# Scattering expert results with an add in the transfer, every slot included

## The chip, the cores and the metric

One core of one Trainium2 chip. The metric is the device time of one execution in microseconds (us). Engines are called by their names; the profile writes PE for TensorE's matrix products (PEld for its weight loads), DVE for VectorE, ACT for ScalarE, POOL for GpSimd and SP for SyncE. "SPq" and "POOLq" are the instructions with which an engine issues transfers.

## The reference

One step of a decoder layer for 512 prompt tokens and 8 sample tokens: a mixer of a recurrent and a convolutional group, attention into 256 memory tokens, and a mixture of experts, each followed by a layer norm. Only the experts matter here:

```python
scores = jax.nn.sigmoid(xf @ w_router)                # 520 tokens, 64 experts
...                                                   # 4 of 8 groups, then the 8 best experts
gates = w_sel / jnp.sum(w_sel, axis=-1, keepdims=True) * ROUTED_SCALE
y = swiglu(xf, w1_s, w3_s, w2_s) + routed_experts(xf, idx, gates, w1_e, w3_e, w2_e)
# routed_experts, for each expert e and the tokens that chose it:
hb = jax.nn.silu(xb @ w1_e[e]) * (xb @ w3_e[e])       # 1024 -> 256
out[token] += (hb @ w2_e[e]) * gate                   # 256 -> 1024
```

All data is float32. Each token has 8 experts, so there are 520 x 8 = 4160 results of 1024 numbers (4 KB), and the output of a token is the sum of its 8.

## The kernel before

The experts are taken one after the other, the fullest first in an order that the kernel works out by sorting. A position of that order is "light" or "heavy" by its number modulo 16 (7 of 16 are light). A light expert has 64 slots for tokens, a heavy one 96, the first of all 112. For each expert e the engines do the following, each engine in a fixed order of steps, with counting semaphores between them:

- VectorE compares each token's place in the expert with the slot numbers (`oh_step`), TensorE multiplies that one-hot matrix with a table (`a_step`), and VectorE turns the product into row numbers (`i_step`: `indices` for heavy experts, `indices_few` for light ones). `picked` holds 8 x token + turn - 8192 for a slot with a token, and 0 for an empty one. `idx_y` is that plus `FAR` = 8192, the row of the result table `y_rows`; `idx_x` is `idx_y` shifted right by 3, the token. An empty slot thus has row 8192, which is beyond both tables, and a transfer with a bounds check leaves it out. For a light expert the results lie in two halves on 128 partitions, and the numbers count half rows.
- GpSimd gathers the tokens' rows with an indirect DMA (`g_step`, L746), in two transfers for a heavy expert (64 and 32 slots).
- TensorE transposes them (L859), multiplies with w1 and w3, later with w2 (L844). ScalarE and VectorE empty the results into `ys`, of which there are two.
- GpSimd scatters `ys` into `y_rows` with an indirect DMA (`s_step`): L759 for heavy experts, again in two transfers, L752 for light ones. Each result has a row of its own, so a plain write does. The last three experts are not scattered; their results are multiplied into the sum at the end.

SyncE loads the weights of expert e+4 as soon as TensorE has used those of expert e (`next_in`, L539 and L540, 1 MB each, after the first products; `next_out`, L544, after the last). There are four buffers, tiles of `arena`. GpSimd's order is: scatter e-1, gather e+3, scatter e, gather e+4; both kinds run on its one queue, q0. A `ys` buffer may be written again when the scatter of two experts earlier has landed (semaphores `m_s`, `m_sm`).

SyncE writes zeros over the rows of `y_rows` early (L555, L557), long before the first scatter. At the end SyncE waits for all scatters (L602 and the line before it), reads `y_rows` back in tiles of 128 tokens, and TensorE adds up the 8 rows of each token with a matrix of ones (`sum_rows`); the last layer norm follows tile by tile.

Of the kernel before, what the change touches and what calls it, by code (L numbers as in the profile page):

```python
# [6 lines left out]
ALU = mybir.AluOpType  # L7
ACT = mybir.ActivationFunctionType
AX = mybir.AxisListType
F32 = mybir.dt.float32  # L10
# [4 lines left out]
P = 128  # L15
D = 1024
# [15 lines left out]
NROW = T * TOPK  # L32
FAR = 8192.0
LCAP = 64
# [5 lines left out]
NB = 16  # L40
# [35 lines left out]
           ("swT", "A"), ("x23", "A"), ("sorted", "V"), ("order", "V"), ("x24", "A"), ("rank", "V"), ("count", "V")]  # L76
GROUPS += [(f"so{t}", "V") for t in range(TT)] + [("slots0", "A"), ("slots1", "A")]
GID = {name: g for g, (name, _) in enumerate(GROUPS)}
SORT_CONSTS = 14 + 2 * NB
FIRST = 4  # L80
LAST_ORDER = [0, 4, 1, 2, 3]
SCATTERED = E - 3
# [68 lines left out]
def decoder_step(nc: bass.Bass, ins, outs):  # L151
# [3 lines left out]
    with ExitStack() as ctx:  # L155
        def sb(name, shape, dt=F32):
            return ctx.enter_context(nc.sbuf_tensor(name, shape, dt))

        def sem(name):
            return ctx.enter_context(nc.semaphore(name))  # L160

        x2_rows = nc.dram_tensor("x2_rows", [T, D], F32)
        q_rows = nc.dram_tensor("q_rows", [NS, D], F32)
        y_rows = nc.dram_tensor("y_rows", [NROW, D], F32)

        arena = sb("arena", [P, 3 * 8192])
        act_mem = sb("act_mem", [P, A_SIZE])
# [11 lines left out]
        h0t = sb("h0t", [P, RC, NS])  # L179
        c8 = sb("c8", [P, 8, RC])  # L180
        eps_t = sb("eps_t", [P, 1])
        small = sb("small", [P, 44])
        order = sb("order", [1, E], I32)
        psum = ctx.enter_context(nc.psum_tensor("psum", [P, 4, D], F32))

# [70 lines left out]
        picked = act_mem[:, A4 + 1820:A4 + 1820 + 2 * NB].rearrange("p (n c) -> p n c", c=2)  # L256
        swT = act_mem[:, A4 + 1296:A4 + 1296 + T]
        gates = act_mem[:, A4 + 1860:A4 + 1860 + 2 * NB].rearrange("p (n c) -> p n c", c=2)
        idx_y = sb("idx_y", [P, NB], U32)
        idx_x = sb("idx_x", [P, NB], U32)  # L260
        more_y = sb("more_y", [CAP - LCAP, NB], U32)
# [35 lines left out]
        wr = gate_w[:, 1, :, :].rearrange("p c n -> p (c n)").rearrange("p (k e) -> p k e", k=KC)  # L297
        rounds_t = small[:, 38:38 + ROUNDS - 1]
        far2 = small[:, 43:44]
        st6 = sb("st6", [P, 2, 6])  # L300
        y_in = [arena[:, 8192 * n:8192 * n + 8192].rearrange("p (s l n) -> p s l n", s=2, l=4) for n in range(3)]
        sum_rows = sb("sum_rows", [P, 2, 2 * TOK])
# [85 lines left out]
        s_sortc = sem("s_sortc")  # L388
# [42 lines left out]
        def emptied(eng, g):  # L431

            who = GROUPS[g][1]
            n = sum(1 for _, w in GROUPS[:g + 1] if w == who)
            eng.wait_ge(s_emA if who == "A" else s_emV, n)
# [25 lines left out]
        def _(sp):  # L461
# [80 lines left out]
            def expert_out(n, e, s):  # L542
                _, wd = ew(n)
                sp.dma_start(wd, I["w2_e"][0, e].rearrange("(p k) n -> p k n", k=2)).then_inc(s, 16)  # L544
# [88 lines left out]
        def _(gp):  # L633
# [66 lines left out]
            def number(out, pattern, base, channel=0):  # L700
                gp.iota(out, pattern=pattern, base=base, channel_multiplier=channel,
                        allow_small_or_imprecise_dtypes=True).then_inc(s_sortc, 1)
# [3 lines left out]
            gp.memset(k64, 64.0).then_inc(s_sortc, 1)  # L706
            number(key_bias, [[-1, E]], E - 1)
            number(expert_no, [[0, 1]], 0, 1)
            both = rank_at.rearrange("p (h i k) -> p h i k", h=2, k=NB)
            for j, k in enumerate(HEAVY):  # L710
                number(both[:, :, :, k], [[0, 2], [len(HEAVY), E // NB]], j)
# [5 lines left out]
            number(slots_m[:, 0:LCAP].rearrange("p (e j) -> p e j", e=LANES), [[1, LANES], [LANES, LCAP // LANES]], 1)  # L717
            number(slots_m[:, LCAP:MCAP].rearrange("p (e j) -> p e j", e=LANES), [[1, LANES], [LANES, MORE // LANES]], LCAP + 1)
            gp.memset(far2, 2 * FAR).then_inc(s_sortc, 1)
            gp.wait_ge(s_sortc, 9 + NB)  # L720
            for k in LIGHT:
                gp.memset(bump[:, k:E:NB], float(CAP - LCAP)).then_inc(s_sortc, 1)
            for k in HEAVY:
# [1 line left out]
            gp.memset(key_bias[:, 0:1], 65536.0).then_inc(s_sortc, 1)  # L725
            gp.memset(key_bias[:, 1:2], 49152.0).then_inc(s_sortc, 1)
            gp.memset(rank_at[0:E, E:2 * E], -1.0).then_inc(s_sortc, 1)
            gp.wait_ge(s_sortc, 12 + 2 * NB)
            gp.memset(rank_at[E:2 * E, 0:E], -1.0).then_inc(s_sortc, 1)
            gp.memset(far2[LCAP:2 * LCAP, :], 2 * FAR + 1).then_inc(s_sortc, 1)  # L730
            gp.wait_ge(s_sortc, SORT_CONSTS)

# [6 lines left out]
            gp.wait_ge(s_x2out, 16 * TT)  # L739

            last_x = gp.to_reg(T - 1)
            last_y = gp.to_reg(NROW - 1)
            last_half = gp.to_reg(2 * NROW - 1)

            def gather(n, b, s, cap=CAP, at=0, idx=idx_x):
                gp.indirect_dma_start(  # L746
# [4 lines left out]
            def scatter_halves(n, src, s):  # L751
                gp.indirect_dma_start(  # L752
                    out=y_rows[:, :].rearrange("r (h n) -> (r h) n", h=2),
                    out_offset=bass.IndirectOffsetOnAxis(ap=idx_y[:, n:n + 1], axis=0),
                    in_=src[:, 0:512], in_offset=None,
                    bounds_check=last_half, oob_is_err=False).then_inc(s, 16)

            def scatter(n, src, s, cap=CAP, at=0, idx=idx_y):
                gp.indirect_dma_start(  # L759
                    out=y_rows[:, :], out_offset=bass.IndirectOffsetOnAxis(ap=idx[0:cap, n:n + 1], axis=0),  # L760
                    in_=src[at:at + cap, :], in_offset=None,
                    bounds_check=last_y, oob_is_err=False).then_inc(s, 16)

            def g_step(e, n):

# [10 lines left out]
            def s_step(e, k, i):  # L776
                n = k % NB
                gp.wait_ge(m_ya, e + 1)
                if not is_light(n):
                    gp.wait_ge(m_yv, len(HEAVY) * i + heavies(k))  # L780
                gp.sem_inc(m_go, 1)
                if is_light(n):
                    scatter_halves(n, ys[:, n % 2, :], m_s[n % 2])
                else:
                    scatter(n, ys[:, n % 2, :], m_s[n % 2], LCAP)
                    scatter(n, ys[:, n % 2, :], m_sm[n % 2], CAP - LCAP if is_big(e) else MORE, LCAP, more_y)
# [49 lines left out]
        def _(pe):  # L836
# [362 lines left out]
            pe.wait_ge(s_late, 9)  # L1199
            pe.wait_ge(s_sortc, SORT_CONSTS)  # L1200
            pe.wait_ge(s_sel, 1)
# [110 lines left out]
            def down_few(b, part):  # L1312
                _, wd = ew(part)
                for k in range(2):
                    for h in range(2):
                        last = mm(psum[LCAP * h:LCAP * h + LCAP, 0, 0:512], hidT[:, b, LCAP * k:LCAP * k + LCAP],
                                  wd[:, k, 512 * h:512 * h + 512], k == 0, k == 1)
                return last
# [517 lines left out]
        def _(dve):  # L1836
            count = [0]

            def chain(ins):

                count[0] += 1
                ins.then_inc(s_v, 1)
                return count[0]
# [21 lines left out]
            y, s, s2, acc = c8[:, 1, :], c8[:, 2, :], c8[:, 3, :], c8[:, 4, :]  # L1865
# [283 lines left out]
            dve.wait_ge(s_ssum, (XH - 1) * 4 + 1)  # L2149
            dve.wait_ge(s_sortc, SORT_CONSTS)  # L2150
            score, biased, left, tmp = R[0], R[1], R[2], R[3]
            sel, share = sw[:, :, 0:E], sw[:, :, E:2 * E]
            link(dve.tensor_tensor(biased, score, rbias.unsqueeze(1).broadcast_to([P, TT, E]), ALU.add))
            for t in range(TT):
                for g in range(8):
                    n = chain(dve.max(rmax[:, t, g, :], biased[:, t, 8 * g:8 * g + 8]))
# [19 lines left out]
            for t in range(TT):  # L2176
                n = chain(dve.max(top8[:, t, :], tmp[:, t, :]))
            dve.wait_ge(s_v, n)
            for t in range(TT):
                n = chain(dve.match_replace(left[:, t, :], top8[:, t, :], tmp[:, t, :], -2e30))  # L2180
# [88 lines left out]
            def indices(n, s, base_count, cap=CAP, split=True, spread=False):  # L2269

                at = 512 * (n % 2)
                dve.tensor_reduce(picked[0:cap, n, :], psum[0:cap, 3, at:at + 6].rearrange("p (v c) -> p v c", v=2), AX.X,
                                  ALU.add).then_inc(s, 1)
                dve.wait_ge(s, base_count + 1)
                if split:
                    dve.tensor_scalar(more_y[0:cap - LCAP, n:n + 1], picked[LCAP:cap, n, 0:1], FAR, None, ALU.add)
                dve.tensor_scalar(idx_y[0:cap, n:n + 1], picked[0:cap, n, 0:1], FAR, None, ALU.add).then_inc(s, 1)
                dve.wait_ge(s, base_count + 2)
                if split:
                    dve.tensor_scalar(more_x[0:cap - LCAP, n:n + 1], more_y[0:cap - LCAP, n:n + 1], 3, None,  # L2280
                                      ALU.logical_shift_right)
                if spread:
                    spread_gates(n)
                return dve.tensor_scalar(idx_x[0:cap, n:n + 1], idx_y[0:cap, n:n + 1], 3, None, ALU.logical_shift_right)  # L2284

            def indices_few(n, s, base_count):

                at = 512 * (n % 2)
                dve.tensor_reduce(picked[:, n, :], psum[:, 3, at:at + 6].rearrange("p (v c) -> p v c", v=2), AX.X,
                                  ALU.add).then_inc(s, 1)  # L2290
                dve.wait_ge(s, base_count + 1)
                dve.tensor_scalar(idx_y[:, n:n + 1], picked[:, n, 0:1], 2.0, far2, ALU.mult, ALU.add).then_inc(s, 1)
                dve.wait_ge(s, base_count + 2)
                return dve.tensor_scalar(idx_x[:, n:n + 1], idx_y[:, n:n + 1], 4, None, ALU.logical_shift_right)

            def hd_few(b):
                return dve.tensor_tensor(silu[:, b, 0:P], silu[:, b, 0:P], psum[:, 2, 512 * b + P:512 * b + 2 * P], ALU.mult)
# [22 lines left out]
            def spread_gates(n):  # L2320

                for h in range(2):
                    dve.tensor_copy(gates[LCAP * h:LCAP * h + LCAP, n, 0:1], picked[0:LCAP, n, 1:2])
                for q in range(4):
                    dve.tensor_copy(gates[MORE * q:MORE * q + MORE, n, 1:2], picked[LCAP:MCAP, n, 1:2])
# [170 lines left out]
```

## Time and profile before

| | us |
|---|---|
| time, median of 2 runs | 1148.35 (1144.96 and 1151.73) |
| the profiled execution | 1147.77 |
| its span, first to last instruction | 1146.0 |
| TensorE busy (products) | 1087.1, 95% of the span |
| VectorE busy | 495.4, 43% |
| ScalarE busy | 288.3, 25% |
| GpSimd busy | 239.4, 21% |
| DMA engines: weight and other SyncE transfers (q1) | 295.64 MB, 64.9% of 16 engines over the span |
| DMA engines: GpSimd's transfers (q0) | 34.94 MB, 8.1% |

Times in rows are us from the start of the span unless marked ns. "share of 16 engines" is the time that packets took, over the time of the 16 DMA engines; it can go a little over 100%, since packets overlap at their ends. A row "DMA to landing" gives the shortest, median and longest time from a transfer's issue to its landing. Shares over the whole span mix stages: the mixer and attention take the first 540 us, the experts the time to about 1086, the sums and the last norm the rest.

### The profile page before, as it was taken

Reading aid. Unit: us, or ns where it says so; the run is one execution under the profiler, and the core shown is the slowest. Engines: PE = TensorE matmul, PEld = TensorE weight load, DVE = VectorE, ACT = ScalarE, POOL = GpSimd, SP = SyncE. Lnnn points to the kernel's source line nnn. Section 1 sums busy time; section 2 is a strip of 40 time slices with the busy share of each in tenths; the row PEclk is TensorE's granted clock in tenths of the full one; section 3 lists DMA queues with packets and bytes.
Section 4 is the critical chain, followed back from the end, with each engine's and each line's share of the span. In section 5 each row is a group of like instructions: output and inputs, shape, how many; then the busy total and the mean of one; then the engine's idle time right before and its main releaser. Section 6 shows DMA issues by size and latency. Waiting matters only on the chain.

```text
span 1146.0 us, 22213 instructions
## 1 busy us (share of the span) xinstructions
PE 1087.1 (95%) x8721; PEld 719.2 (63%) x8721; DVE 495.4 (43%) x1429; ACT 288.3 (25%) x615; POOL 239.4 (21%) x296
## 2 busy tenths in 40 slices
PE   7999998999997989989999999999999999999996
PEld 6888665877884757847555555555556555565531
DVE  0349999234028444681323333233343333433236
ACT  1112163004033041411223222232232322323220
POOL 3120040000000001031333333333333333343200
PEclk9999999999999999999999999999999999999999
DMA  9630315016034859875999999999999999999696
GB/s 331 271 147 1 147 32 183 1 67 243 2 136 137 316 207 419 357 302 213 385 401 407 415 408 417 404 407 414 408 415 411 405 418 404 403 420 396 239 385 261
DMA packets 71026, 336.27 MB, mean 293 GB/s; under 512 B 10951, under 2 KB 17311, under 8 KB 44301
## 3 DMA queue, kind: packets, MB, share of 16 engines
q1 hardware_dynamic: 55461, 295.64, 64.9%
q0 software_dynamic: 14048, 34.94, 8.1%
q10 hardware_dynamic: 1424, 4.35, 1.0%
q8 instruction: 70, 1.15, 0.4%
q14 instruction: 23, 0.19, 0.0%
HBM read 299.36 MB, written 44.70 MB: 300 GB/s over the span
## 4 chain that ended last, share of the span: by engine, by line
PE 72%; DVE 17%; DMA 6%; issue 2%; ACT 2%; SPq 0%; POOL 0%; DVEq 0%; ACTq 0%; POOLq 0%
PE psum L844 64%; PE psum L859 8%; DVE act_mem L1882 7%; DVE mk_mem L2047 2%; DMA arena<-y_rows 2%; DMA arena<-in_w_in_dram 2%; DMA mk_mem<-x_rows,idx_x 2%; DMA act_mem<-x_rows,idx_x 1%; DVE act_mem L2103 0%; ACT act_mem L1647 0%; DVE act_mem L2254 0%; DVE act_mem L1982 0%; ACT act_mem L1656 0%; DVE act_mem L2266 0%; POOL y_rows L759 0%
## 5 line engine op out<-in xcount | busy, mean ns | idle before, releaser
L844 PE MATMUL psum<-arena,act_mem 128*32 128x128 f32 (+6 forms) x5488 | 493.4, 365 | 2.1 <-ACT act_mem L1762 1.1
L844 PEld LDWEIGHTS psum<-arena,act_mem 128*32 128x32 f32 (+4 forms) x5488 | 254.8, 121 | 192.2 <-issue 96.7
L844 PE MATMUL psum<-act_mem,arena 128*128 128x260 f32 (+1 forms) x1472 | 328.5, 386 | 8.9 <-DMA arena<-in_w_o_dram 3.7
L844 PEld LDWEIGHTS psum<-act_mem,arena 128*128 128x128 f32 x1472 | 281.6, 196 | 53.4 <-DMA arena<-in_w_o_dram 4.6
L859 PE MATMUL psum<-ident,act_mem 128*128 128x128 f32 (+6 forms) x488 | 79.2, 291 | 17.1 <-DMA act_mem<-in_x_prompt_dram 4.5
L759 POOL DMA_INDIRECT y_rows<-act_mem,idx_y x35 | 39.2, 1120 | 242.3 <-DVE act_mem L2317 219.4
L2315 DVE COPY act_mem<-psum 64x512 f32<-64x512 f32 x35 | 24.2, 693 | 126.8 <-PE psum L844 126.8
L1882 DVE SCALAR_TENSOR_TENSOR act_mem<-act_mem,wcb 128x511 f32<-128x511 f32 (+29 forms) x120 | 77.8, 737 | 0.1
L859 PEld LDWEIGHTS psum<-ident,act_mem 128*128 128x128 f32 (+6 forms) x488 | 57.2, 168 | 30.5 <-issue 15.9
L844 PEld LDWEIGHTS psum<-act_mem 128*96 128x96 bf16 (+5 forms) x419 | 29.9, 124 | 58.2 <-issue 55.4
L2308 DVE SCALAR_TENSOR_TENSOR act_mem<-act_mem,psum 128x128 f32<-128x128 f32 x35 | 12.2, 348 | 114.3 <-ACT act_mem L1718 114.3
L1714 ACT ACTIVATE act_mem<-psum 128x768 f32<-128x768 f32 (+1 forms) x63 | 45.1, 715 | 57.1 <-PE psum L859 57.1
L844 PE MATMUL psum<-act_mem 128*96 128x6 bf16 (+7 forms) x419 | 56.5, 263 | 2.0 <-ACT act_mem L1737 1.3
L1718 ACT ACTIVATE act_mem<-psum 128x192 f32<-128x192 f32 x35 | 11.6, 331 | 162.6 <-PE psum L844 162.6
L859 PE MATMUL psum<-ident,mk_mem 128*128 128x128 f32 (+4 forms) x316 | 43.8, 281 | 7.3 <-issue 4.5
L859 PEld LDWEIGHTS psum<-ident,mk_mem 128*128 128x128 f32 (+4 forms) x316 | 36.9, 183 | 19.2 <-issue 16.3
L752 POOL DMA_INDIRECT y_rows<-act_mem,idx_y x26 | 26.7, 1026 | 95.8 <-ACT act_mem L1753 53.0
L844 PE MATMUL psum<-arena,kv_mem 128*128 128x512 f32 x96 | 41.8, 594 | 1.2 <-ACT kv_mem L1537 1.2
L1743 ACT ACTIVATE act_mem<-psum 64x512 f32<-64x512 f32 x35 | 20.7, 590 | 77.1 <-PE psum L844 77.1
L682 POOL MEMSET act_mem<- 128x512 f32 x1 | 0.5, 524 | 184.1 <-PE psum L859 184.1
L759 POOL DMA_INDIRECT y_rows<-act_mem,more_y x35 | 34.6, 989 | 10.7 <-DVE idx_x L2284 5.8
L1504 ACT ACTIVATE act_mem<-psum,par 128x520 f32<-128x520 f32 x24 | 16.1, 695 | 77.0 <-PE psum L844 76.9
(288 smaller groups left out, 886.3 us busy)
## 6 DMA issues: line engine op xcount, KB each, us to landing
arena<-in_w_e_dram SPq DMA_DIRECT2D x192, 1024.0 KB, 10.4
y_rows<-tail SPq DMA_DIRECT2D x1, 16384.0 KB, 55.3
arena<-y_rows SPq DMA_DIRECT2D x8, 2048.0 KB, 20.7
arena<-in_w_in_dram SPq DMA_DIRECT2D x16, 512.0 KB, 17.8
arena<-in_cache_mem_k_dram SPq DMA_DIRECT2D x8, 1024.0 KB, 8.5
arena<-in_cache_mem_v_dram SPq DMA_DIRECT2D x8, 1024.0 KB, 11.9
arena<-in_w_v_dram SPq DMA_DIRECT2D x1, 4096.0 KB, 24.4
arena<-in_w_k_dram SPq DMA_DIRECT2D x1, 4096.0 KB, 13.9
```

The source lines that it names most:

```text
L752: gp.indirect_dma_start(out=y_rows[:, :].rearrange("r (h n) -> (r h) n", h=2), out_offset=bass.IndirectOffsetOnAxis(ap=idx_y[:, n:n + 1], ...
L759: gp.indirect_dma_start(out=y_rows[:, :], out_offset=bass.IndirectOffsetOnAxis(ap=idx[0:cap, n:n + 1], axis=0), in_=src[at:at + cap, :], i ...
L844: return pe.matmul(out, lhsT, rhs, start=first, stop=last)
L859: return pe.transpose(out, in_, ident[0:n, 0:n])
L1504: act.activation(out, two(bank(name)), func, **kw).then_inc(s_emA, 1)
L1714: return act.activation(xgT[:, b, :, 0:cap], psum[:, 1, :].rearrange("p (k s) -> p k s", k=KC)[:, :, ROWS_AT:ROWS_AT + cap], ACT.Copy)
L1718: return act.activation(silu[:, b, 0:192], psum[:, 2, 512 * b:512 * b + 192], ACT.Silu)
L1743: act.activation(out[0:LCAP, 0:512], psum[0:LCAP, 0, 0:512], ACT.Copy)
L1882: return dve.scalar_tensor_tensor(out, in0, w, in1, ALU.mult, ALU.add)
L2047: ins = dve.tensor_tensor_reduce(junk, kc[:, m, XD * h:XD * h + XD], q_all[:, b, XD * h:XD * h + XD], 1.0, 0.0, ALU.mult, ALU.add, ss[:, m ...
L2308: dve.scalar_tensor_tensor(silu[:, b, 0:P], silu[:, b, 0:P], gates[:, n, 0:1], psum[:, 2, 512 * b + 192:512 * b + 320], ALU.mult, ALU.mult)
L2315: dve.tensor_copy(out[0:LCAP, 512:1024], psum[LCAP:2 * LCAP, 0, 0:512])
```

## The change

The scatter is done with an add in the transfer: the DMA engines fetch the row of `y_rows`, add the row of `ys` to it and write it back. The rows that results go to hold zeros, so the sums are the same. Empty slots are no longer left out: `y_rows` gets 256 spare rows behind its 4160, and the index of a slot is the smaller one of its row number and a spare row that belongs to its partition and to the parity of the expert (`spare` for rows, `spare2` for half rows, two new columns each in `small`). Nobody reads the spare rows. The gather still leaves empty slots out, since a spare row divided by 8 is beyond the last token. The light experts' indices take one more VectorE instruction; the heavy ones' get a second operation in the instruction that is there.

```diff
-SORT_CONSTS = 14 + 2 * NB
+SORT_CONSTS = 14 + 2 * NB + 2
...
-        y_rows = nc.dram_tensor("y_rows", [NROW, D], F32)
+        y_rows = nc.dram_tensor("y_rows", [NROW + 2 * P, D], F32)
...
+        spare = small[:, 44:46]
+        spare2 = small[:, 46:48]
...
+            number(spare, [[P, 2]], NROW, 1)
+            number(spare2, [[2 * P, 2]], 2 * NROW, 1)
...
-            last_y = gp.to_reg(NROW - 1)
-            last_half = gp.to_reg(2 * NROW - 1)
+            last_y = gp.to_reg(NROW + 2 * P - 1)
+            last_half = gp.to_reg(2 * (NROW + 2 * P) - 1)
...
                     out=y_rows[:, :].rearrange("r (h n) -> (r h) n", h=2),
                     out_offset=bass.IndirectOffsetOnAxis(ap=idx_y[:, n:n + 1], axis=0),
                     in_=src[:, 0:512], in_offset=None,
-                    bounds_check=last_half, oob_is_err=False).then_inc(s, 16)
+                    bounds_check=last_half, oob_is_err=True, compute_op=ALU.add).then_inc(s, 16)
...
                     out=y_rows[:, :], out_offset=bass.IndirectOffsetOnAxis(ap=idx[0:cap, n:n + 1], axis=0),
                     in_=src[at:at + cap, :], in_offset=None,
-                    bounds_check=last_y, oob_is_err=False).then_inc(s, 16)
+                    bounds_check=last_y, oob_is_err=True, compute_op=ALU.add).then_inc(s, 16)
...
                 if split:
-                    dve.tensor_scalar(more_y[0:cap - LCAP, n:n + 1], picked[LCAP:cap, n, 0:1], FAR, None, ALU.add)
-                dve.tensor_scalar(idx_y[0:cap, n:n + 1], picked[0:cap, n, 0:1], FAR, None, ALU.add).then_inc(s, 1)
+                    dve.tensor_scalar(more_y[0:cap - LCAP, n:n + 1], picked[LCAP:cap, n, 0:1], FAR, spare[LCAP:cap, n % 2:n % 2 + 1], ALU.add, ALU.min)
+                dve.tensor_scalar(idx_y[0:cap, n:n + 1], picked[0:cap, n, 0:1], FAR, spare[0:cap, n % 2:n % 2 + 1], ALU.add, ALU.min).then_inc(s, 1)
...
                 dve.wait_ge(s, base_count + 2)
-                return dve.tensor_scalar(idx_x[:, n:n + 1], idx_y[:, n:n + 1], 4, None, ALU.logical_shift_right)
+                dve.tensor_scalar(idx_x[:, n:n + 1], idx_y[:, n:n + 1], 4, None, ALU.logical_shift_right)
+                return dve.tensor_scalar(idx_y[:, n:n + 1], idx_y[:, n:n + 1], spare2[:, n % 2:n % 2 + 1], None, ALU.min)
```

## Rows read from the trace of the kernel before

**Rows 1.** The page's slices: 40 equal parts of the span; busy share in tenths.

```profile
PE   7999998999997989989999999999999999999996
...
DMA  9630315016034859875999999999999999999696
```

**Rows 2.** Table by stage, 800 to 900 us: busy us by engine, clock, DMA.

```profile
800.00:900.00 100.00, 99.93 (x1097) 57.78 (x1100) 33.45 (x129) 28.17 (x71) 35.19 (x35) 1.00 1.02 410
```

**Rows 3.** Chain that ended last, 800 to 840 us: start, duration, engine, line, instructions.

```profile
806.69 1.08 PE psum L859 x8
...
811.01 5.76 PE psum L844 x96
...
826.11 1.09 PE psum L859 x8
...
838.78 5.73 PE psum L844 x96
```

**Rows 4.** DMA view, 600 to 1000 us: queue, packets, MB, share of 16 engines.

```profile
q1 hardware_dynamic: 19114, 139.18, 85.0%
q0 software_dynamic: 9452, 23.98, 15.5%
```

**Rows 5.** Weights, issue to landing: stretches from 560, 800 and 900 us.

```profile
DMA to landing us min/median/max: 8.5/12.1/13.9
...
DMA to landing us min/median/max: 7.0/10.1/12.7
...
DMA to landing us min/median/max: 6.9/9.7/11.7
```

**Rows 6.** Timeline, 800 to 822 us: start, duration, engine, line, operation.

```profile
806.88 0.34 SPq L539 DMA_DIRECT2D arena<-in_w_e_dram  x1
...
807.31 0.38 SPq L540 DMA_DIRECT2D arena<-in_w_e_dram  x1
...
812.93 0.15 DVE L2294 TENSOR_SCALAR idx_x<-idx_y 128x1 uint32<-128x1 uint32 x1
...
813.29 1.40 POOL L759 DMA_INDIRECT y_rows<-act_mem,idx_y  x1 [5.92 <-DVE act_mem L2317]
...
816.19 0.96 POOL L746 DMA_INDIRECT mk_mem<-x_rows,idx_x  x1 [0.30 <-issue]
```

**Rows 7.** Gathered rows, issue to landing, 800 to 900 us.

```profile
DMA to landing us min/median/max: 5.7/7.2/9.1
```

**Rows 8.** Waits, 560 to 1146 us: total us, times, longest.

```profile
PEld psum L859 <- DMA act_mem<-x_rows,idx_x: 3.0, 3, 1.6
```

**Rows 9.** DMA view, 540 to 1086 us.

```profile
q0 software_dynamic: 12960, 32.44, 15.5%
```

**Rows 10.** GpSimd's instructions by line and form, 540 to 1146 us.

```profile
L759 POOL DMA_INDIRECT y_rows<-act_mem,idx_y x35 | 39.2, 1120 | 242.3 <-DVE act_mem L2317 219.4 <-DVE act_mem L2328 23.0
L759 POOL DMA_INDIRECT y_rows<-act_mem,more_y x35 | 34.6, 989 | 10.7 <-DVE idx_x L2284 5.8 <-issue 4.9
L746 POOL DMA_INDIRECT mk_mem<-x_rows,idx_x x30 | 28.9, 965 | 9.5 <-issue 9.5
L746 POOL DMA_INDIRECT act_mem<-x_rows,idx_x x30 | 28.9, 964 | 9.4 <-issue 9.4
L752 POOL DMA_INDIRECT y_rows<-act_mem,idx_y x26 | 26.7, 1026 | 95.8 <-ACT act_mem L1753 53.0 <-DVE idx_x L2294 39.0 <-issue 3.8
```

**Rows 11.** GpSimd's timeline ahead of the stage, idle time before the instruction.

```profile
492.13 0.14 POOL L734 IOTA small<- 128x5 f32 x1 [43.21 <-PE psum L859]
```

**Rows 12.** Waits of SyncE's DMA queue, whole span.

```profile
SPq L607 <- DMA y_rows<-act_mem,more_y: 8.4, 1, 8.4
...
SPq L602 <- DMA y_rows<-act_mem,idx_y: 4.5, 1, 4.5
```

**Rows 13.** Chain that ended last, its last DMA.

```profile
1109.15 25.54 DMA arena<-y_rows
```

**Rows 14.** Result table, issue to landing, 1000 to 1085 us.

```profile
DMA to landing us min/median/max: 2.2/6.9/7.4
```

More of the change, by code:

```diff
@@ L181, in decoder_step @@
         eps_t = sb("eps_t", [P, 1])
-        small = sb("small", [P, 44])
+        small = sb("small", [P, 48])
         order = sb("order", [1, E], I32)
@@ L719, in _ @@
             gp.memset(far2, 2 * FAR).then_inc(s_sortc, 1)
-            gp.wait_ge(s_sortc, 9 + NB)
+            gp.wait_ge(s_sortc, 11 + NB)
             for k in LIGHT:
@@ L727, in _ @@
             gp.memset(rank_at[0:E, E:2 * E], -1.0).then_inc(s_sortc, 1)
-            gp.wait_ge(s_sortc, 12 + 2 * NB)
+            gp.wait_ge(s_sortc, 14 + 2 * NB)
             gp.memset(rank_at[E:2 * E, 0:E], -1.0).then_inc(s_sortc, 1)
```

## The prediction

> **What bounds the kernel now.** Start with the row of slices: TensorE and the DMA engines are both full from slice 19 on, which is the expert stage, about 540 to 1086 us [rows 1]. Everything the change touches lies there, so the question is which of the two sets the pace. The table by stage says TensorE: 99.9 of 100 us busy at full granted clock [rows 2]. The chain that ended last says the same: in the stage it runs from one TensorE group to the next with hardly a gap [rows 3]. The DMA view is the second thing to look at, because it decides what the change costs. Between 600 and 1000 us the weight queue q1 takes 85.0% of the 16 engines and the GpSimd queue q0, which carries gathers and scatters, 15.5% [rows 4]. That is 100.5%, so no engine time is left. TensorE is still ahead by a hair: a weight transfer landed 12.1 us after its issue at the start of the stage and 9.7 us after it near the end [rows 5], so the backlog drains by 2.4 us in some 370. The two resources are balanced to within 1%, with DMA a little faster, and work added to the DMA engines has no idle room to go into. It has only the lead that prefetching has built up.
>
> **How long the lead is.** Take one expert, X. Its first products end at 806.69, where the transposes of the next expert's rows begin [rows 3], and the two loads of up-weights for X+4 are issued at 806.88 and 807.31 [rows 6]. The products of X+1 start at 811.01; two experts come between, and those of X+4 start at 838.78 [rows 3]. A load issued at 807.31 that needs the longest landing of that stretch, 12.7 us [rows 5], is there at 820.0 and needed at 838.8: 19 us of cover. It is spent once, not per expert. When it is gone, TensorE runs at the pace of the DMA engines. With the 2 us that the drain shows, I count 21 us.
>
> **The gathers have less cover.** The gather for X+3 is issued at 816.19 [rows 6]; the median landing of gathers in this stretch is 7.2 us, the longest 9.1 [rows 7], so it is there at 823.4, in the worst case 825.3, for transposes that start at 826.11 [rows 3]: 2.7 us, or 0.8. TensorE already waits for gathers now and then [rows 8].
>
> **The change part by part.**
>
> *Removed:* nothing that takes time; the plain write becomes an add.
>
> *Rows.* In 540 to 1086 us q0 moved 32.44 MB in 15.5% of the engines' time [rows 9], which is 0.155 x 546 = 84.6 us of all 16 engines. In it lie 60 gathers (30 and 30) and 61 scatters (35 and 26) [rows 10]. An expert's gather and its scatter move the same rows of 4096 B, so 32.44 MB / 4096 = 7,920 rows over 121 transfers are 65.5 rows each; the scatters have 3,990 rows and 42.6 us. Before, a slot without a token points beyond the table and no row is moved. After, each slot is moved: 26 light experts x 64 row equivalents (128 half rows), 34 heavy ones x 96, and the first with 112, in all 5,040 rows, 1.263 times as many. If an add cost what a write does, that is 53.8 us, 11.2 more.
>
> *The add.* No row of this trace shows one, so I bound it. From below: the table's row is fetched and added under the transfer's own time, a price of 1 write, with a gain excluded because the bytes written are no fewer. From above: the fetch, the source's read and the write go one after the other, a price of 3. The nearest rows are the two kinds that q0 has now. A gather row brings 4 KB out of HBM, a scatter row takes 4 KB from SBUF there, and an add has to do both; by the shared 15.5% each is one row's price. So I take 2. The scatters then need 2 x 53.8 = 107.6 us, 65.0 more. At 1 it is 11.2 more and at 3 118.8 more.
>
> What rows 9 and 10 can't tell is whether the two reads of an add share a time slot. The Trainium skill, "Collectives: The Full Stack", section "The bandwidth ceiling: the fold count and why AG ≠ RS ≠ AR", says that a reducing transfer is slower than a copying one because it puts two reads on the same read ring, and not because of the adding, and gives a measured ratio of 1.93. By that price the scatters would need 103.8 us, 61 more, and the forecast below would be 1190. No run here shows it yet.
>
> *What of it reaches the end.* With no idle engine time, 65.0 us of DMA work less 21 us of cover leave 44 us by which the stage becomes longer. TensorE's work is unchanged; it waits for weights, or for gathers.
>
> *The index arithmetic.* A heavy expert's two index instructions get a second operation, no more instructions. A light expert gets one more on VectorE, of a kind that takes 0.15 us (the shift at 812.93 [rows 6]), 28 times, 4 us in all. It holds up the semaphore that lets GpSimd gather: 812.93 + 0.15 + 0.15 = 813.2 in place of 813.1, for a gather at 816.19 [rows 6]. The scatter in front of it, at 813.29, hides it. VectorE is a third busy [rows 2], and what queues behind it is the next expert's table of slots, which is needed several us later. So 0; without that cover 4 us, and as much again for the heavy ones if a second operation costs a whole instruction.
>
> *The constants.* Two more number tables on GpSimd before the stage, a fraction of a us each. GpSimd then stands idle for 43.2 us [rows 11], so 0.
>
> *GpSimd's issue.* The transfers take 0.96 to 1.12 us of GpSimd each whether they have 32, 64 or 128 indices [rows 10], so the spare indices cost nothing there. If an add took twice as long to issue, heavy experts' gathers would leave 2 us later, within the 2.7 us above when the landing is a median one, and beyond the 0.8 us when not.
>
> *The tail.* The last scatter's landing holds up the first read of the table by SyncE (4.5 and 8.4 us of waiting at the two lines [rows 12]; the reads that follow end the chain with 25.5 us of DMA [rows 13]). The shortest landing of a scatter, with the weights gone, is 2.2 us [rows 14]. With a fetch ahead of the write and 96 rows for some 65 it may be 0 to 5 us longer; I take 2.
>
> **Sum.** 65.0 - 21 + 2 = 46 us. Against the profiled execution, 1147.8 us (span 1146.0 plus 1.8 around it, 0.6 us under the median of the two runs shown), that is 1194 us, 4.0% slower. Ends: at a price of 1 the 11.2 us vanish in the cover, 1148 to 1153 with the tail; at 3 it is 118.8 - 21 + 5 = 103, 1251.
>
> **Rivals.** A measurement of this kernel tells about 2% from no change, 23 us.
>
> A. *The add is hidden in the transfer*, or the add isn't done as such: the same time as a plain write to all slots. For it: no row shows that a fetch takes engine time beside a write that goes on anyway. Against it: the engines have no idle time left [rows 4], and each row that q0 brings in now takes as long as one that it takes out. Time 1148 to 1153, not slower. It decides where 42.6 x (1.263 f - 1) - 21 + 2 stays under 23 us, so for a price f under 1.57.
>
> B. *An add costs three rows or more, or holds up the gathers behind it.* Scatter and gather share the queue q0, and I take it that a gather doesn't overtake. A heavy expert's scatter goes from about 65 rows to 96 adds. If q0 gets half of the engines while it has work (an estimate: it gets 15.5% on average and comes in bursts), 65 rows now take 65 x 0.0107 x 2 = 1.4 us, and 96 adds at 2 take 4.1 us: 2.7 us later, just the cover of a median gather. A gather that is late by 2 us costs those 2 us once in two experts at least (the gather for X+3 is issued after the results of X-1), 60 us in all; but in that case TensorE asks for weights more slowly and the DMA bound above falls away, so the larger counts, not the sum. Time 1225 to 1260 or above.
>
> C. *Faster.* Without slots beyond the table GpSimd may build its transfers a little quicker; but GpSimd stands before nearly each heavy scatter waiting for VectorE, and a quarter of a us there changes nothing behind it. 1140 to 1148.
>
> **Chances.** Forecast, price near 2 and DMA the pace (1171 to 1225): 0.50. A: 0.27. B: 0.20. C: 0.03, of which 0.01 for some larger gain that I don't see. So faster 0.01, same 0.29, slower 0.70. The range goes from the lower end of A to just short of the far end of B: 1148 to 1245. The forecast's own range, by prices from 1.6 to 2.5, is 1171 to 1222.
>
> **What will show it.** In the profile after: DMA share still full over the whole stage with fewer GB/s of weights per us (q1 under 85%, q0 near 25%), q0's bytes up by a quarter for the scatters or by more if the fetched rows are counted, weights landing up to 20 us or more after issue in place of 10, TensorE busy 92 to 94% in place of 99%, waiting for arena<-in_w_e. If it waits for x_rows instead, rival B's second half holds. If weights still land after 10 us and TensorE stays at 99%, A holds. The clock of TensorE should stay at full; long waits in the stage that lower it would add to the time. The forecast is wrong if engines count an add's read as free (A), if the adds are moved one at a time, or if the cover is larger than I read from one expert.

## The result and the profile after

| | before | changed |
|---|---|---|
| time, median (us) | 1148.35 (1144.96, 1151.73) | 1198.49 (1197.94, 1199.03) |
| the profiled execution, its span | 1147.77, 1146.0 | 1197.94, 1196.1 |
| TensorE busy | 1087.1 | 1098.1 |
| first read of the result table by SyncE | 1085.48 | 1135.81 |

The ratio is 1.0437, 95% interval 1.030 to 1.057. The time from the first read of the table to the end of the span is the same (60.5 and 60.3 us), so the whole loss lies in the expert stage and in the landing of its last scatter. Lines of `kernel.py` from 300 on are 2 to 5 higher in the changed kernel: L844 became L848, L859 L863, L759 L763, L752 L756, L746 L750.

The page's slices, and the table by stage for 800 to 900 us:

```profile
PE   7999998999988898988998998998999999999995
...
DMA  9630404034048399669999999999999999999796
```

```profile
800.00:900.00 100.00, 90.01 (x1018) 52.33 (x1014) 31.89 (x126) 24.62 (x63) 42.26 (x35) 1.00 1.03 382
```

The engines' row is as full as in [rows 1], but TensorE has fallen from 99.9 to 90.0 us in the hundred [rows 2], and the GB/s from 410 to 382. The DMA view, first of 600 to 1000 us, then of the stage up to SyncE's first read (540 to 1136 us), shows who has taken the time:

```profile
q1 hardware_dynamic: 17557, 127.87, 77.7%
q0 software_dynamic: 9782, 24.46, 24.5%
```

```profile
q1 hardware_dynamic: 25371, 184.65, 75.6%
q0 software_dynamic: 14624, 36.59, 25.2%
```

q1 has gone from 85.0% to 77.7% and q0 from 15.5% to 24.5% [rows 4]. Over the stage q0 needs 0.252 x 596 = 150.2 us of all 16 engines where it needed 84.6 [rows 9]: 65.6 us more, against 65.0 in the prediction. Its bytes rose by 4.15 MB, the spare slots; the rows that an add fetches are not in this count.

Where TensorE waits is a different thing. Its waits ahead of the transposes (L863), from 560 us on:

```profile
PE psum L863 <- issue: 28.6, 15, 3.4
...
PEld psum L863 <- DMA mk_mem<-x_rows,idx_x: 17.0, 9, 3.3
...
PEld psum L863 <- DMA act_mem<-x_rows,idx_x: 13.2, 8, 2.7
...
PE psum L863 <- DMA mk_mem<-x_rows,idx_x: 8.3, 5, 2.9
PE psum L863 <- DMA act_mem<-x_rows,idx_x: 7.9, 6, 2.1
```

There is no wait for weights among them, and from 560 us to the first read of the table PE never stands idle ahead of the products that read weights (L848). (PE's waits are the same ones seen once more, after those of its weight loads, so the two are not added: 30.2 us at the loads, where [rows 8] and a wait of 0.5 us stood before; PE itself stood idle ahead of the transposes for 44.8 us, 8.5 before, most of it as "issue", for which the profile names no releaser.) The landings say why: first weights in 900 to 1000 us, then gathered rows in 800 to 900.

```profile
DMA to landing us min/median/max: 14.9/16.1/18.0
```

```profile
DMA to landing us min/median/max: 7.8/9.0/10.2
```

Weights land 6 us later than before [rows 5], far from the 19 us that would make them late. The gathers land 1.8 us later [rows 7], and the chain that ended last now runs through them:

```profile
800.85 1.36 POOL y_rows L763
...
802.51 9.43 DMA mk_mem<-x_rows,idx_x
811.94 0.84 issue
812.78 1.13 PE psum L863 x8
```

Read from above: GpSimd issues the second part of a heavy scatter, then the first part of a heavy gather, which lands 9.43 us later. For the 0.84 us after it ("issue") the profile names no releaser, but TensorE waits for both parts of a heavy gather, and the second part left later:

```profile
803.81 0.94 POOL L750 DMA_INDIRECT mk_mem<-x_rows,more_x  x1 [0.30 <-issue]
```

It landed 8.9 us after its issue, at 812.7, and the transposes begin at 812.78. The waits stand at one kind of place. Of the 60 experts from the fifth on, 19 are heavy ones whose gather is issued behind a heavy expert's scatter. Ahead of their transposes TensorE stood idle for 40.0 us, ahead of the other 41 for 4.8. Before, it was 8.3 and 0.2: these gathers had hardly any cover even then, under 0.9 us for 18 of the 19. One second part in the kernel before:

```profile
799.74 0.93 POOL L746 DMA_INDIRECT act_mem<-x_rows,more_x  x1 [0.31 <-issue]
```

It landed after 6.8 us, at 806.5, for transposes that start at 806.69 [rows 3].

GpSimd's own rows have grown as well [rows 10]:

```profile
L763 POOL DMA_INDIRECT y_rows<-act_mem,idx_y x35 | 58.5, 1671 | 263.5 <-DVE act_mem L2322 240.7 <-DVE act_mem L2333 22.8
L763 POOL DMA_INDIRECT y_rows<-act_mem,more_y x35 | 47.5, 1358 | 10.7 <-issue 10.7
L756 POOL DMA_INDIRECT y_rows<-act_mem,idx_y x26 | 41.3, 1587 | 74.9 <-ACT act_mem L1757 40.3 <-DVE idx_y L2299 34.6
```

### The profile page after: what moved, and what is told of

Its sections match the earlier page's. It is cut to its first block, busy times and chain, and to the rows that moved or that the text cites. A ratio compares the mean times of both kernels' runs of the same rounds, so it can differ in the third digit from the quotient of the medians.

```text
span 1196.1 us, 22243 instructions
## 1 busy us (share of the span) xinstructions
PE 1098.1 (92%) x8721; PEld 721.0 (60%) x8721; DVE 502.0 (42%) x1457; ACT 288.3 (24%) x615; POOL 288.2 (24%) x298
## 3 DMA queue, kind: packets, MB, share of 16 engines
HBM read 299.36 MB, written 44.70 MB: 288 GB/s over the span
## 4 chain that ended last, share of the span: by engine, by line
PE 52%; DVE 20%; DMA 18%; issue 6%; POOL 2%; ACT 2%; SPq 0%; DVEq 0%; POOLq 0%; ACTq 0%
PE psum L848 46%; DMA act_mem<-x_rows,idx_x 8%; DVE act_mem L1886 7%; DMA mk_mem<-x_rows,idx_x 6%; PE psum L863 6%; DVE mk_mem L2051 2%; DMA arena<-y_rows 2%; POOL y_rows L763 2%; DMA arena<-in_w_in_dram 1%; DVE act_mem L2322 1%; DVE act_mem L2330 1%; DVE act_mem L2107 0%; ACT act_mem L1651 0%; DVE idx_y L2281 0%; DVE act_mem L2258 0%
## 5 line engine op out<-in xcount | busy, mean ns | idle before, releaser
L848 PE MATMUL psum<-arena,act_mem 128*32 128x128 f32 (+6 forms) x5488 | 499.9, 368 | 2.1 <-ACT act_mem L1766 1.1
L848 PEld LDWEIGHTS psum<-arena,act_mem 128*32 128x32 f32 (+4 forms) x5488 | 255.3, 121 | 199.3 <-issue 103.9
L848 PE MATMUL psum<-act_mem,arena 128*128 128x260 f32 (+1 forms) x1472 | 328.3, 386 | 8.6 <-DMA arena<-in_w_o_dram 3.7
L848 PEld LDWEIGHTS psum<-act_mem,arena 128*128 128x128 f32 x1472 | 280.8, 196 | 53.7 <-DMA arena<-in_w_o_dram 4.5
L763 POOL DMA_INDIRECT y_rows<-act_mem,idx_y x35 | 58.5, 1671 | 263.5 <-DVE act_mem L2322 240.7
L863 PE MATMUL psum<-ident,act_mem 128*128 128x128 f32 (+6 forms) x488 | 81.4, 296 | 38.8 <-issue 16.9
L863 PEld LDWEIGHTS psum<-ident,act_mem 128*128 128x128 f32 (+6 forms) x488 | 58.3, 169 | 53.2 <-issue 26.9
L863 PE MATMUL psum<-ident,mk_mem 128*128 128x128 f32 (+4 forms) x316 | 45.2, 287 | 22.7 <-issue 11.7
L848 PEld LDWEIGHTS psum<-act_mem 128*96 128x96 bf16 (+5 forms) x419 | 29.9, 124 | 58.2 <-issue 55.4
L756 POOL DMA_INDIRECT y_rows<-act_mem,idx_y x26 | 41.3, 1587 | 74.9 <-ACT act_mem L1757 40.3
L863 PEld LDWEIGHTS psum<-ident,mk_mem 128*128 128x128 f32 (+4 forms) x316 | 38.1, 184 | 34.9 <-DMA mk_mem<-x_rows,idx_x 17.0
L848 PE MATMUL psum<-act_mem 128*96 128x6 bf16 (+7 forms) x419 | 56.5, 262 | 1.9 <-ACT act_mem L1741 1.3
L763 POOL DMA_INDIRECT y_rows<-act_mem,more_y x35 | 47.5, 1358 | 10.7 <-issue 10.7
L848 PE MATMUL psum<-arena,kv_mem 128*128 128x512 f32 x96 | 41.8, 593 | 1.2 <-ACT kv_mem L1541 1.2
L750 POOL DMA_INDIRECT act_mem<-x_rows,idx_x x32 | 31.9, 996 | 15.1 <-issue 9.4
```

Source lines behind the costliest of these rows:

```text
L750: gp.indirect_dma_start(out=xg[b][at:at + cap, :], out_offset=None, in_=x2_rows[:, :], in_offset=bass.IndirectOffsetOnAxis(ap=idx[0:cap, n ...
L756: gp.indirect_dma_start(out=y_rows[:, :].rearrange("r (h n) -> (r h) n", h=2), out_offset=bass.IndirectOffsetOnAxis(ap=idx_y[:, n:n + 1], ...
L763: gp.indirect_dma_start(out=y_rows[:, :], out_offset=bass.IndirectOffsetOnAxis(ap=idx[0:cap, n:n + 1], axis=0), in_=src[at:at + cap, :], i ...
L848: return pe.matmul(out, lhsT, rhs, start=first, stop=last)
L863: return pe.transpose(out, in_, ident[0:n, 0:n])
```

## The experiments

Two theories were put against each other. T: the engines' time sets the pace of the stage, and a wait for a gather is only where that shows. L: the gathers come late because the way from a scatter to the next gather is longer, in issue and in landing; engine time isn't the limit. Times are medians; the kernel before, run beside them on the same chips, took 1148.0 to 1149.1.

**The two parts alone.** e1 keeps the add and leaves empty slots out (of its edits, those for heavy experts; the light ones' are alike):

```diff
-                    bounds_check=last_y, oob_is_err=True, compute_op=ALU.add).then_inc(s, 16)
+                    bounds_check=last_y, oob_is_err=False, compute_op=ALU.add).then_inc(s, 16)
...
-                dve.tensor_scalar(idx_y[0:cap, n:n + 1], picked[0:cap, n, 0:1], FAR, spare[0:cap, n % 2:n % 2 + 1], ALU.add, ALU.min).then_inc(s, 1)
+                dve.tensor_scalar(idx_y[0:cap, n:n + 1], picked[0:cap, n, 0:1], FAR, None, ALU.add).then_inc(s, 1)
```

> The add alone: the transfers add, but empty slots are left out as before, with no spare rows and no extra index instruction. Theory T (the DMA engines' time sets the pace of the expert stage, and the waits for gathers are only the place where it shows): the scatters' 42.6 us double, 42.6 us more work; the changed kernel turned 65 us more work into 48 us more stage, so 17 us were covered, and this one should be 26 us longer in the stage and 2 in the tail, 1174 to 1178. Theory L (the gathers come late because they stand behind a scatter that takes longer to issue and to move; engine time is not the limit): the issue of a scatter by GpSimd is as long as in the changed kernel and a heavy scatter still doubles, so most of the loss stays, 1180 to 1192.

Measured: 1182.8, ratio 1.030 (1.027 to 1.034). That is above T's range and in L's: the 17 us of cover that T carried over from the changed kernel were too many. The price of an add, though, comes out clean, since the rows are those of before. The DMA view of e1, 540 to 1118 us (its first read of the table), and GpSimd's first heavy scatter:

```profile
q0 software_dynamic: 14624, 32.45, 22.4%
```

```profile
L763 POOL DMA_INDIRECT y_rows<-act_mem,idx_y x35 | 57.3, 1638 | 249.5 <-DVE act_mem L2321 226.5 <-DVE act_mem L2332 23.0
```

The bytes are those of [rows 9] to 0.01 MB; the time is 0.224 x 578 = 129.5 us in place of 84.6. The scatters' 42.6 us became 87.5: an add costs 2.05 writes. Single packets of 4 KB on q0 say the same without a split between gathers and scatters: in the trace of e1 a plain one took 159 ns, one with an add 327 ns (medians).

e2 keeps the spare rows and writes plainly (the light experts' scatter too):

```diff
-                    bounds_check=last_y, oob_is_err=True, compute_op=ALU.add).then_inc(s, 16)
+                    bounds_check=last_y, oob_is_err=True).then_inc(s, 16)
```

> The spare rows alone: every slot is written, with a plain write and no add. T: 11 us more DMA work, less than the cover, 1148 to 1153. L: a heavy expert's scatter moves 96 rows in place of some 65 to 75, so gathers behind it come up to 0.7 us later and use up part of their 2.7 us of cover, 1149 to 1156. If the issue time on GpSimd stays at about 1.0 us, the longer issue of the changed kernel belongs to the add; if it rises to 1.4, to the spare slots.

Measured: 1157.2, ratio 1.0056 (1.003 to 1.008), more than either expected, for 11 us of work. A part of that is not the edit's. The profiled execution's span is 11.4 us longer than the one before, and 5.5 of these are there already when SyncE writes the zeros (422.2 us in place of 416.7), ahead of all that the edit touches: the granted clock of the first 440 us was 0.97 in place of 0.99. From the issue of the first scatter to that of the last one's second part, called stage time from here on, it took 549.4 us in place of 544.2, and these 5 us stand where the add's do: TensorE was idle for 13.7 us in place of 8.3 ahead of heavy gathers behind heavy scatters. (The profiled executions of e6 to e9 and e12 also reach the first gather late, by 2.5 to 4.3 us. So stage times of the profiled executions stand beside the medians where few us count. They are compared only between kernels with the same order of gathers and scatters.) The issue of the first heavy scatter is back near the length of before (1120 ns [rows 10]), so the longer issue belongs to the add:

```profile
L763 POOL DMA_INDIRECT y_rows<-act_mem,idx_y x35 | 41.0, 1170 | 244.7 <-DVE act_mem L2322 221.9 <-DVE act_mem L2333 22.8
```

**Gathers first.** e3 and e4 swap the two steps in GpSimd's loops, in the changed kernel and in the one before:

```diff
-                    s_step(NB * i + (k - 1), k - 1, i)
                     g_step(NB * i + (k + 3), (k + 3) % NB)
+                    s_step(NB * i + (k - 1), k - 1, i)
```

> The changed kernel, but GpSimd issues the gather of expert e+3 ahead of the scatter of expert e-1 in place of behind it. T: the DMA work is the same; TensorE waits for weights where it waited for gathers, and at most what is left of the 21 us of cover comes back: 1184 to 1198. L: gathers leave about 3 us earlier, more than the 2.9 us that TensorE waited for one, so nearly the whole loss comes back: 1148 to 1162.

Measured: 1192.3, ratio 1.038 (1.036 to 1.040), as T had it: 6 us of 50 came back. Waits for gathers are gone, and what the prediction had described comes into sight, the lead of the weights being used up. Landings of weights in 560 to 600, 640 to 680 and 900 to 1000 us, then PE's longest entry in the list of waits, then the table by stage:

```profile
DMA to landing us min/median/max: 13.5/17.5/20.4
...
DMA to landing us min/median/max: 25.9/30.7/33.8
...
DMA to landing us min/median/max: 23.4/30.8/36.5
```

```profile
PE psum L848 <- issue: 33.8, 25, 4.2
```

```profile
600.00:700.00 100.00, 99.10 (x1102) 58.19 (x1098) 35.69 (x135) 27.81 (x70) 41.71 (x35) 1.00 1.03 378
700.00:800.00 100.00, 91.06 (x946) 55.66 (x944) 29.68 (x115) 24.32 (x62) 37.39 (x31) 0.95 1.03 382
```

Until 700 us TensorE is at 99%, while the landing climbs to some 31 us, which is the time from issue to need (31.5 by the rows of expert X). Then the cover is gone, TensorE drops to 91% and its granted clock falls below full in parts of the stage. The profile names no releaser for these waits; that they are for weights is read from their place, ahead of the products that read weights, and from one that can be followed: a load issued at 679.1 landed after 33.8 us, at 712.9, and TensorE, idle for 3.07 us, started its products at 712.93.

> The kernel before, with the gather issued ahead of the scatter. T: TensorE and the DMA engines are balanced, nothing or a few us: 1143 to 1148. L: the 8.7 us of waits for gathers go, and nothing takes their place: 1138 to 1142.

Measured: 1142.7, ratio 0.995 (0.993 to 0.997): faster than both kernels by a small but clear margin. TensorE has no gap left between 800 and 900 us:

```profile
800.00:900.00 100.00, 100.00 (x1142) 58.41 (x1142) 34.67 (x130) 28.00 (x70) 32.22 (x34) 1.00 1.02 415
```

**Room on the engines.** e5 and e6 load only the first half of the second weight matrix from the fifth expert on:

```diff
-                sp.dma_start(wd, I["w2_e"][0, e].rearrange("(p k) n -> p k n", k=2)).then_inc(s, 16)
+                sp.dma_start(wd[:, 0:k, :], I["w2_e"][0, e].rearrange("(p k) n -> p k n", k=2)[:, 0:k, :]).then_inc(s, 16)
```

> The kernel before with less DMA work: from the fifth expert on only the first half of the second weight matrix is loaded, and the products use an older second half, so the result is not the reference's. The first queue needs 453 us for 184 MB in the expert stage; 60 half megabytes less are 77 us less. T and L alike: TensorE alone sets the pace, and gathers land a little sooner, 1138 to 1147. It is the base for the next one.

> The changed kernel with the same loads left out (so again not the reference's result). T: the engines have 77 us of room for the 65 us that the adds and the spare slots take, and 2 us remain in the tail: 0 to 8 us above the kernel before with the same loads left out. L: the longer issue on GpSimd (1.67 and 1.36 us for a heavy expert's two scatters in place of 1.12 and 0.99) and the doubled rows ahead of each gather stay, and 25 us or more of the 50 are left.

Measured: 1143.6 and 1172.6. T by itself fails here: 29 us are left, as L had it. In e6 weights land early (a median of 8.8 us in 800 to 900), but the chain is a loop of two experts that never touches them:

```profile
781.67 1.12 PE psum L863 x8
782.78 2.91 PE psum L848 x24
...
786.61 0.42 DVE act_mem L2322
...
787.91 0.22 DVE idx_y L2281
...
790.04 1.37 POOL y_rows L763
...
791.72 8.15 DMA mk_mem<-x_rows,idx_x
799.87 0.87 issue
800.74 1.13 PE psum L863 x8
```

From one expert's transposes (781.67) to those of the expert two later (800.74) it takes 19.1 us, of which TensorE works 17.4: the second product of the heavy expert before it, its results, the indices, two scatters, the landing of the gather's two parts (the second, issued at 793.01, after 7.6 us, in the row called "issue"), and again. Gathers land after 8.6 us in e6, after 6.5 in e5.

**Both eased.** e9 is e6 with gathers first; e10 is e6 with one scatter of 96 rows in place of 64 and 32:

```diff
-                    scatter(n, ys[:, n % 2, :], m_s[n % 2], LCAP)
-                    scatter(n, ys[:, n % 2, :], m_sm[n % 2], CAP - LCAP if is_big(e) else MORE, LCAP, more_y)
+                    scatter(n, ys[:, n % 2, :], m_s[n % 2], CAP if is_big(e) else MCAP)
+                    gp.sem_inc(m_sm[n % 2], 16)
```

> The changed kernel with both bounds eased: gathers ahead of scatters, and half of the second weight matrix not loaded from the fifth expert on (not the reference's result). With only the loads cut, the changed kernel kept 29 us of its loss over the plain kernel with the same cut (1172.6 against 1143.6), with only the gathers first 43. If the loss has two bounds, the engines' time and the way from a scatter to the next gather, and nothing else, both gone leave 0 to 8 us over 1143.6: 1144 to 1152. If T alone were right, with too little room made by the cut, gathers first would change nothing here: 1166 to 1173. If some third cost of the add is left, it shows as the rest.

Measured: 1145.8, 2.2 above e5. Its stage time is 534.2 us, that of e4 534.5. TensorE is busy throughout, adds and spare rows notwithstanding:

```profile
800.00:900.00 100.00, 100.00 (x1112) 58.22 (x1110) 35.66 (x135) 28.02 (x71) 41.33 (x34) 1.00 1.02 362
```

> The changed kernel with the loads cut (not the reference's result), gathers behind scatters, and a heavy expert's 96 slots scattered in one transfer in place of two, with the same rows. It takes one issue, 1.36 + 0.30 us, out of the way from the results to the gather of each heavy expert and leaves the rows as they are. If the longer issue makes the gathers late, more than half of the 29 us goes: 1145 to 1158. If the doubled rows in front of the gather in its queue do, little goes: 1164 to 1173.

Measured: 1149.2. One issue of 1.66 us less takes 23 of the 29 us; the landing of gathers fell with it, from 8.6 to 7.2 us (medians of 800 to 900 us), so the edit does not part issue and landing altogether.

> The changed kernel with all loads, gathers behind scatters, and one transfer in place of two for a heavy expert's scatter. With the loads cut this edit took 23 of 29 us. If the engines' time sets the pace here, as the run with gathers first had it (1192), it brings back no more than that one did: 1190 to 1195. If the late gathers were the larger part of the 50 us, it goes below 1180.

Measured, with all loads: 1195.1, ratio 1.043 (1.041 to 1.045). The edit that took 23 us where the engines had room takes 3 where they have none. The gathers left earlier and landed later, after 9.3 us in place of 9.0.

**The cover.** e7 and e8 are e1 and e2 with gathers first:

> Gather ahead of scatter, with the add on the slots that have a token alone. It tells what the lead of the weights is worth where TensorE doesn't wait for gathers; with gathers first the plain kernel took 1142.7 and the changed one 1192.3, so 65 us of work became 49.6. If the lead covers a fixed 15 us or so once, then 43 us of work become 27, 1168 to 1172. If a fixed share of the work is hidden (0.76 of it shows), 1174 to 1177.

> Gather ahead of scatter, with plain writes to every slot. A fixed cover of some 15 us takes in all of the 11 us, 1142 to 1145; a fixed share leaves 8.5 us, 1149 to 1153.

Measured: 1174.8 and 1147.9. Over e4 that is 32.1 us for the add alone and 5.2 for the spare rows alone, and 49.6 for both (e3); the work is 44.9 and 65.6 by the DMA views and, for the spare rows alone, 9.5 (17.3% of 542 us in e8, 15.7% of 537 in e4, where the prediction's rows gave 11.2). What stays hidden is 13, 4 and 16 us, neither a fixed amount nor a fixed share, though the first lies in the range of the share. But the medians take in what comes behind the last scatter. The stage time (one execution each) is 534.5 us in e4, 534.5 in e8, 560.4 in e7 and 576.4 in e3: up to the last scatter all of the 9.5 us were hidden, 19 of the 44.9 and 24 of the 65.6, the last two close to the 21 us of cover in the prediction. Most of the rest of the loss comes behind it. From the last scatter's issue to the first read of the table 2.2 us pass in e4, and 6.5, 7.2 and 7.9 in e8, e7 and e3, the kernels in which more of the weights' lead had been used (landings of 17.7, 23.0, 30.3 and 30.8 us, medians of 800 to 900).

> The kernel before with gathers first and one scatter for a heavy expert, plain writes. TensorE was busy 99.3% or more of each 100 us of the stage with gathers first alone (1142.7), so the shorter issue finds nothing to shorten: 1141 to 1144, still faster than the kernel before by 0.4 to 0.7%.

Measured: 1144.5, ratio 0.998 (0.997 to 0.999). Nothing is gained over e4, half a us outside what was expected.

## Why the prediction was right, and where it was not

Forecast 1194, measured 1198.5, for a reason that holds in size and was named at the wrong place.

*Rows.* 1.263 times as many: by the bytes, 32.44 + 4.15 MB, the scatters' 16.35 MB became 20.5, 1.25 times. Right.

*The add.* A price of 2 against 2.05 (e1). The ratio of 1.93 that the Trainium skill gives ("Collectives: The Full Stack", "The bandwidth ceiling: the fold count and why AG ≠ RS ≠ AR") for collectives is 6% under it; the trace agrees with its order of size, and can't show that it is the read ring. The sum of work, 65.0 us, was measured as 65.6.

*What of it reaches the end.* This is the step that failed in its mechanism: "TensorE waits for weights" and the 21 us of cover. The last part of the last scatter was issued 48.3 us later (1083.26 and 1131.52), so 17 us were hidden, but the lead of the weights was not spent: TensorE waited for gathers first, 30 us at its weight loads. I had read the gathers' cover, 2.7 us, from one gather [rows 6], and that one is a light expert's, in one part. I let a longer issue and a slower landing each fit into it alone. They came together: 0.9 us of issue for a heavy expert's two scatters on the mean and 1.8 us of landing; and the 19 heavy gathers behind heavy scatters had hardly any cover to take them: their second part leaves 1.3 us after the first, and TensorE already stood idle ahead of nine of them before. That the hidden 17 us are near the 21 of the sum is luck, as far as the changed kernel goes; the 21 themselves were read about rightly, as the kernels with gathers first show (19 and 24). This is the second half of rival B, and the sentence that went with it ("the larger counts, not the sum") is what the runs show:

| medians, us; in brackets the stage time | all loads | loads cut |
|---|---|---|
| plain, gathers behind | 1148.35 (544.2) | 1143.6 (e5; 540.4) |
| changed, gathers behind | 1198.5 (591.9) | 1172.6 (e6; 560.2) |
| plain, gathers first | 1142.7 (e4; 534.5) | no run |
| changed, gathers first | 1192.3 (e3; 576.4) | 1145.8 (e9; 534.2) |

With the way to the gather eased, the engines' time alone costs 49.6 us (e3 over e4; 41.9 of it in the stage time); with the engines eased, the way to the gather alone costs 29.0 (e6 over e5; 19.9); with both eased 2.2 are left (e9 over e5, none of it in the stage time beside e4; the plain kernel with both eased has no run); with neither it is 50.1 (47.7). Gathers behind scatters cost 6 us in the plain kernel and 6 in the changed one. So T sets the time in the changed kernel, and L decides that gathers, and not weights, are what TensorE is seen waiting for.

*Index arithmetic, constants.* Nothing: in e9 the same instructions leave TensorE at 100%.

*The tail.* 2 us: the last scatter's second part lay 2.2 us before SyncE's first read, now 4.3 (1131.52 to 1135.81); with both bounds eased it is 4.2 in e9, and 2.2 in e5 with plain writes.

*GpSimd's issue.* I took 0 and named what twice the length would do. It became 1.4 to 1.6 times as long, with the add and not with the spare slots (e1, e2). In the kernel as changed this costs little, in one with room on the engines most of 29 us.

*TensorE's clock.* It was to stay full; the granted clock was 0.97 to 1.00 in the hundreds of the stage (0.94 in 540 to 600), between full and six stretches at the lower of its two levels, 1.2 GHz, each around the end of a wait of TensorE of 1.9 to 3.4 us, and TensorE was busy 11 us longer with the same instructions. (Before, the longest wait of the stage was 1.3 us and the clock stayed full.) Where the engines set the pace this would come out of TensorE's waits; no run shows it apart.

*The range.* By the prediction's own sum, prices of 1.6 and 2.5 give 1172 and 1221, a us off the ends that it states.

*Rival A* is ruled out by e1. *Open:* what hides some of the work with gathers behind scatters, where the weights' lead is not spent: by stage time 18 us in the changed kernel, 14 in e1, 4 in e2. The shares of q0 and q1 add up to 98.5% of the stage before and to 100.8% after, which is 13 us; weights landing 4 to 6 us later account for some of the rest. Why the hidden part grows with the work was not settled.

## What to carry to other kernels

A wait that ends last in a stage with two full resources names a place, not the cause: ease it alone and see whether the time moves (6 of 50 us here). Read the cover of a kind of transfer from the ones that land last before their use: it was 2.7 us for the gather at hand, and under 0.9 us for 18 others. When a transfer is made to add, price it as two transfers of the same rows on the engines, and look at what is queued behind it on its own queue. In this kernel the loads that are needed soonest belong ahead of the stores that nobody waits for, which made the plain kernel 0.5% faster (e4).

## What the runs showed of the hardware that was not expected

- The busy share of the DMA engines doesn't tell whether they set the pace. It reads 1.02 to 1.03 in every hundred us from 600 to 1000 us of e9, at some 360 GB/s with TensorE at 100%, and 1.03 in e3, where TensorE waits for weights. Neither the GB/s nor the HBM bytes of the page count the rows that an add fetches (299.36 MB read, before and after).
- An indirect transfer with an add took GpSimd 1.36 to 1.67 us to issue, a plain one 0.99 to 1.12, for the same number of indices (e1 and e2: it is the add, not the number of rows moved).
- The chain names the landing of a gather's first part and calls the 0.8 to 1.2 us after it "issue". Where the second part's landing can be read, it fills that time: TensorE starts 0.1 us after it (812.7 and 812.78 in the trace after).
